# Experts' weights of a mixture-of-experts stage: transfers of 1 MB into twelve slots in place of 2 MB into six pairs of slots

## The reference, cut to what matters

```python
def moe(h, router_w, router_b, w1, w3, w2):
    ...
    out = gates[:, 0:1] * swiglu(t, w1[0], w3[0], w2[0])
    for e in range(1, N_EXPERTS):
        out = out + gates[:, e:e + 1] * swiglu(t, w1[e], w3[e], w2[e])
```

## Time and profile before

| | us |
|---|---|
| median of 3 runs | 1326.77 |
| lowest and highest | 1325.58, 1328.07 |
| the profiled execution | 1325.2 |
| its span, first to last instruction | 1323.4 |

### The profile page before, as it was taken

One profiled execution on the slowest core, in us unless ns is written; L12 is line 12 of the kernel. 1 busy time (PEld: TensorE's weight loads), 2 busy tenths in 40 slices (PEclk: granted clock), 3 DMA queues, 4 the chain that ended last, 5 costly groups with the idle time before them and its releaser, 6 DMA issues.

```text
span 1323.4 us, 40419 instructions
## 1 busy us (share of the span) xinstructions
PE 1225.4 (93%) x19184; PEld 918.4 (69%) x19184; DVE 354.2 (27%) x641; ACT 228.7 (17%) x307; POOL 17.8 (1%) x33
## 2 busy tenths in 40 slices
PE   4999999999989799999999999998779999999675
PEld 4889999999979768986555666664445666665343
DVE  3658664555454431001100000010001010001022
ACT  2434352333332210011000001000000000000001
POOL 0200000000000000000000000000000000000100
PEclk8999999999999799999999999999999999999999
DMA  9957678654556779999999999999999999999993
GB/s 387 356 188 285 270 298 330 260 178 176 188 223 257 285 280 405 403 410 429 424 426 425 424 425 424 425 424 427 426 425 425 425 419 417 415 414 415 425 425 165
DMA packets 44149, 470.73 MB, mean 356 GB/s; under 512 B 5140, under 2 KB 7736, under 8 KB 9544
## 3 DMA queue, kind: packets, MB, share of 16 engines
q1 hardware_dynamic: 42192, 462.83, 85.1%
q0 software_dynamic: 1392, 4.89, 1.1%
q10 hardware_dynamic: 392, 0.35, 0.1%
HBM read 463.99 MB, written 4.06 MB: 354 GB/s over the span
## 4 chain that ended last, share of the span: by engine, by line
PE 79%; DMA 16%; DVE 2%; issue 1%; ACT 1%; ACTq 0%; SPq 0%; POOL 0%; DVEq 0%; POOLq 0%
PE ps L485 78%; DMA raw<-moe_stream 14%; DMA raw<-dense_stream 1%; DMA hT<-in_norm_g 1%; DVE w_lo L1286 1%; PE ps L596 0%; ACT w_hi L1096 0%; PE ps L498 0%; PE ps L670 0%; DVE hT L1374 0%; DVE xT L1405 0%; ACTq L1108 0%; DVE tok L1814 0%; PE ps L908 0%; DVE xT L1535 0%
## 5 line engine op out<-in xcount | busy, mean ns | idle before, releaser
L485 PE MATMUL ps<-raw,hg 128*32 128x256 f32 x9408 | 522.3, 381 | 28.3 <-DMA raw<-moe_stream 28.3
L485 PEld LDWEIGHTS ps<-raw,hg 128*32 128x32 f32 x9408 | 326.7, 110 | 216.0 <-DMA raw<-moe_stream 22.3
L485 PE MATMUL ps<-rnd,w_hi 128*128 128x256 f32 x1632 | 299.8, 286 | 7.4 <-DVE rnd L1386 4.3
L485 PE MATMUL ps<-raw,arena 128*32 128x256 f32 x4704 | 265.2, 383 | 20.7 <-DMA raw<-moe_stream 20.7
L485 PEld LDWEIGHTS ps<-rnd,w_hi 128*128 128x128 f32 x1632 | 256.6, 194 | 11.4 <-issue 7.4
L485 PEld LDWEIGHTS ps<-raw,arena 128*32 128x32 f32 x4704 | 167.4, 111 | 114.1 <-issue 17.9
L485 PE MATMUL ps<-rnd,w_lo 128*128 128x256 f32 x816 | 232.5, 285 | 0.0
L1741 DVE TENSOR_TENSOR arena<-ps,arena 64x768 f32<-64x768 f32 (+1 forms) x48 | 41.3, 860 | 644.7 <-ACT arena L1209 644.7
L485 PEld LDWEIGHTS ps<-rnd,w_lo 128*128 128x128 f32 x816 | 158.1, 194 | 0.0
L1286 DVE TENSOR_TENSOR w_lo<-raw,w_hi 128x2048 fp32r<-128x2048 f32 x53 | 121.2, 2291 | 111.2 <-ACT w_hi L1096 111.2
L1209 ACT ACTIVATE arena<-ps 64x768 f32<-64x768 f32 (+1 forms) x56 | 40.4, 722 | 631.9 <-PE ps L485 631.9
(11 more groups left out here) (175 smaller groups left out, 402.9 us busy)
## 6 DMA issues: line engine op xcount, KB each, us to landing
raw<-moe_stream SPq DMA_DIRECT2D x168, 2048.0 KB, 22.3
raw<-dense_stream SPq DMA_DIRECT2D x101, 1024.0 KB, 7.9
y_rows<-arena SPq DMA_DIRECT2D x20, 96.0 KB, 13.0
out<-tok SPq DMA_DIRECT2D x2, 512.0 KB, 3.3
arena<-dft_constants POOLq DMA_DIRECT2D x1, 640.0 KB, 9.8
tok<-in_x_prompt SPq DMA_DIRECT2D x1, 512.0 KB, 4.6
tok<-in_x_sample SPq DMA_DIRECT2D x1, 512.0 KB, 5.7
arena<-bias_table POOLq DMA_DIRECT2D x1, 512.0 KB, 11.4
```

The costliest lines, as they stand in the source:

```text
L485: return pe.matmul(out, lhsT, rhs, start=first, stop=last, **kw)
```

## The change

The twelve slots are filled one by one: each piece is a transfer of its own, with a semaphore of its own. A piece's slot can be loaded again when that piece is used. In memory each piece is stored by itself, so that each partition reads 8 KB in one run. The order of slots in the buffers is the same as before, and so is the order of pieces. The first two pieces take the place of the first pair in the dense part, and the wait for the dense loads in `raw` is made slot by slot. The stores of result rows stand after the thirteenth transfer of a job, which is piece 12; before, they stood after the pair of pieces 12 and 13.

```diff
-PAIR = 2
-PAIR_SLOTS = 6
-RING = PAIR * PAIR_SLOTS
-MOE_LOADS = MOE_PIECES // PAIR
+RING = 12
...
-    moe_full = [sem(f"moe_full{i}") for i in range(PAIR_SLOTS)]
+    moe_full = [sem(f"moe_full{i}") for i in range(RING)]
...
+    RAW_ORDER = (4, 5, 0, 1, 2, 3)
...
-    def pair_slot(t):
-
-        k = t % PAIR_SLOTS
-        if k < PAIR_SLOTS // 2:
-            at = (2, 0, 4)[k]
-            return raw_2[:, at:at + PAIR, :]
-        at = (4, 0, 2)[k - PAIR_SLOTS // 2]
-        return raw[:, at:at + PAIR, :]
+    def piece_slot(t):
+
+        k = t % RING
+        return raw_2[:, (2, 3, 0, 1, 4, 5)[k], :] if k < RING // 2 else raw[:, RAW_ORDER[k - RING // 2], :]
...
-                t = MOE_LOADS * job + i // PAIR
-                pe.wait_ge(moe_full[t % PAIR_SLOTS], 16 * (t // PAIR_SLOTS + 1))
-                return pair_slot(t)[:, i % PAIR, :].rearrange("p (i n) -> p i n", i=2)
+                t = MOE_PIECES * job + i
+                pe.wait_ge(moe_full[t % RING], 16 * (t // RING + 1))
+                return piece_slot(t).rearrange("p (i n) -> p i n", i=2)
...
-                sp.dma_start(pair_slot(0), moe_stream[0, 0]).then_inc(moe_full[0], 16)
+                for t in range(2):
+                    sp.dma_start(piece_slot(t), moe_stream[t, 0]).then_inc(moe_full[t], 16)
...
-            for i in range(0 if job else 1, MOE_LOADS):
-                t = MOE_LOADS * job + i
-                if t < PAIR_SLOTS // 2:
+            for i in range(0 if job else 2, MOE_PIECES):
+                t = MOE_PIECES * job + i
+                if t < RING // 2:
                     sp.wait_ge(*used_up[N_SPLIT - 1])
-                elif t < PAIR_SLOTS:
+                elif t < RING:
                     for n in range(N_PRE - RAW, N_PRE):
-                        if n % RAW // PAIR * PAIR == (4, 0, 2)[t - PAIR_SLOTS // 2]:
+                        if n % RAW == RAW_ORDER[t - RING // 2]:
                             sp.wait_ge(*raw_free[n])
-                sp.wait_ge(e_used, PAIR * (t + 1))
-                piece = moe_stream[i, bass.ds(which, 1)].rearrange("o p a b n -> (o p) a b n") if e else moe_stream[i, 0]
-                sp.dma_start(pair_slot(t), piece).then_inc(moe_full[t % PAIR_SLOTS], 16)
-                if e and job < EXPERTS and i == PAIR_SLOTS:
+                sp.wait_ge(e_used, t + 1)
+                piece = moe_stream[i, bass.ds(which, 1)].rearrange("o p n -> (o p) n") if e else moe_stream[i, 0]
+                sp.dma_start(piece_slot(t), piece).then_inc(moe_full[t % RING], 16)
+                if e and job < EXPERTS and i == RING:
                     store_rows(job - 1)
...
-    moe = np.empty((MOE_LOADS, EXPERTS, P, PAIR, 2, HALF // 2), np.float32)
+    moe = np.empty((MOE_PIECES, EXPERTS, P, 2, HALF // 2), np.float32)
...
-        piece = moe[i // PAIR, :, :, i % PAIR]
+        piece = moe[i]
...
-    return pre, moe
+    return pre, moe.reshape(MOE_PIECES, EXPERTS, P, HALF)
```

More of the change, by code:

```diff
@@ L171 @@
 LAST_DOWN = max(n for n, piece in enumerate(PLAN) if piece[0] == "w2")
-assert MOE_PIECES % PAIR == 0 and len(MOE_PLAN) == MOE_PIECES
+assert len(MOE_PLAN) == MOE_PIECES
 ROWS = 4
```

## The result

The changed kernel takes 1331.55 us (median of 20 runs, 1328.15 to 1333.98); the kernel before, 20 runs beside it, 1326.74. The ratio is 1.0034, 95% interval 1.0027 to 1.0042: slower by 4.8 us. Predicted were 1333.0 us and +6.3. The profiled execution has a span of 1328.7 us, 5.3 more than before.

A forecast was written before the change was run, and what follows sets the result against it. Transfers were taken to bound the kernel from 585 us to the last landing at 1307.67 us. Terms +10.1 - 2.0 - 1.85 = +6.3 us gave 1333.0 us, range 1325.0 to 1338.0.

The forecast's parts named there:

- Row length: From 585 us to the last landing, 8 KB rows instead of 16 KB cost 1.4% of 722 us, +10.1 us.
- early dense window: In 12:36 us of the profile before, 8 KB rows of the dense stream saturated the engines at 420 GB/s.
- One transfer-bound stretch of 722 us: From 585 to 1307.67 us, the last landing, transfers set the pace throughout, in long jobs as in light ones.
- Slots one by one: In the first expert, slots returned one piece earlier let transfers run closer behind TensorE: -2.0 us, bounds 0 and -4.9.
- Tail: After the last landing TensorE has one piece left instead of two: -1.85 us, bound above 0.
- SyncE's work: 168 more issues at 0.40 us cost SyncE 67 us, inside its waits for TensorE of 739.9 us; priced at nothing.
- The cover: SyncE's 739.9 us of waits for TensorE hide the added issues; without it they would cost 67 us.
- B: Gain and loss cancel: short rows cost 0.2 to 0.9%, or less of the stretch counts; 1324.3 to 1329.4 us, chance 0.22.
- C: Row length costs nothing, so the lead and half tail remain: -3.85 us, 1322.9 us, chance 0.12.
- D: Each transfer's own cost comes through: 5% of a lone pair's 3.1 us uncovered gives 1349 us; chance 0.05.
- B's second half: Dips of slices 31 to 35 are a true TensorE limit, so 1.4% is lost over 557 us only, +7.8.
- C's rule: The Trainium skill asks for 128 partitions and at least 1 MiB per DMA for full bandwidth; both kernels keep to that.

The follow-up runs named there:

- The part alone: Kernel before with only the rows shortened: 168 transfers of 2 MB in pairs of slots, each partition's 16 KB as two 8 KB runs; 1337.26 us, ratio 1.0073.
- the pair kernels: Kernel before with first 56 pieces one by one, then 16 KB pairs; ratio 0.9990, with last pair one by one too 0.9972, with last six 0.9952.

## Why the prediction was right, step by step

**Row length, +10.1 us.** Shown. The part alone lengthened the stage by 10.9 us and the time by 9.8. In the changed kernel the windows fell from 427 to 420 and from 426 to 419 GB/s, as the row of the early dense window had said. The 1.4% was my choice between 0, 1.7 and 2.1%, and it was a good one: from 124 us after the stage's start to the last landing the mean is 419 GB/s before and 413 after.

**One transfer-bound stretch of 722 us.** Held as a whole: the 10.9 us that short rows alone added are 1.5% of it, and four of the seven later jobs are long ones. Had the long jobs kept TensorE's own pace, only the light ones would have grown, by under 5 us (an estimate: 1.6% of some 300 us). But the loss is not even. Before, then after, and the two deep dips after beside a calm stretch:

```profile
600.00:1300.00 700.00, 652.70 (x11680) 389.67 (x11680) 73.19 (x93) 46.64 (x66) 3.85 (x4) 0.99 1.00 422
600.00:1060.00 460.00, 435.26 (x7768) 259.93 (x7768) 42.86 (x56) 31.39 (x46) 0.00 (x0) 0.99 1.01 425
1060.00:1225.00 165.00, 164.00 (x3044) 98.97 (x3036) 16.12 (x20) 10.02 (x13) 0.00 (x0) 1.00 1.00 416
...
600.00:1300.00 700.00, 650.19 (x11606) 377.26 (x11605) 71.93 (x90) 46.16 (x65) 3.85 (x4) 1.00 1.01 417
600.00:1060.00 460.00, 435.87 (x7762) 254.41 (x7765) 42.88 (x56) 31.45 (x46) 0.00 (x0) 1.00 1.01 419
1060.00:1225.00 165.00, 162.11 (x2988) 96.22 (x2978) 14.73 (x18) 9.88 (x13) 0.00 (x0) 1.00 1.01 413
671.30:701.30 30.00, 30.00 (x560) 18.07 (x556) 3.86 (x4) 2.41 (x3) 0.00 (x0) 1.00 1.01 418
1102.60:1132.60 30.00, 30.00 (x560) 18.07 (x556) 3.86 (x4) 2.41 (x3) 0.00 (x0) 1.00 1.00 398
1211.40:1241.40 30.00, 22.31 (x372) 11.07 (x364) 4.04 (x6) 1.77 (x3) 3.46 (x4) 1.00 1.01 400
```

Up to 1060 us the rate falls by 1.4%, in the 165 us of the dips by 0.7%.

**Slots one by one, -2.0 us.** Right in kind and rather small. Between short rows in pairs and the changed kernel the stage shrinks by 3.5 us (2.3 against the second trace of the changed kernel), and 1.07 MB more is moved at the end of the first expert, 2.5 us. In the pair kernels the term was 2.3 to 2.9 us of stage. A piece landed 7.4 us after its issue in the median of 480:570 us, where I had said 7.6:

```profile
L1022 SPq DMA_DIRECT2D raw<-moe_stream x35: 327/328/356, 479.8 to 568.0; - x35
...
DMA to landing us min/median/max: 6.0/7.4/8.4
```

**Tail, -1.85 us.** 3.80 to 1.98, -1.82. It holds only because the transfers ahead of the last are single as well and TensorE waits for each of them. The prediction had only asked whether the piece before the last lands in time.

The measured terms give 10.9 - 3.5 - 1.8 = +5.6 against +6.3 predicted, +5.3 in the span (0.3 us less in the dense part) and +4.8 in the medians. That the sum came out so near is in part luck: I had the row term 0.8 us too small and the slots 0.3 to 1.5 us too small, and these two errors have opposite signs in it.

**SyncE's work, nothing.** The price was right as far as the runs show, its working was not: I had 0.40 us for each issue and 67 us in all. The wait of SyncE for TensorE fell from 739.9 us by far more:

```profile
SPq L1022 <- PE ps L479: 383.6, 217, 15.2
```

Most of those 356 us lie in issues that take longer: all expert issues together took 57 us before and 382 after. They cost the transfers no rate that the runs show: in 920:980 it is 420 GB/s with issues of 1992 ns in the median, and 420 with pairs of short rows, whose issues take 373 ns there.

```profile
L1022 SPq DMA_DIRECT2D raw<-moe_stream x37: 332/1992/4349, 904.8 to 992.0; - x37
...
L1031 SPq DMA_DIRECT2D raw<-moe_stream x12: 372/373/373, 922.8 to 979.0; - x12
```

So most of the 6% that the chain gives to SPq is time in which the engines were full anyway. The cover held, but it was half used up, not an eleventh.

**Against the rivals.** B (gain and loss cancel), C (row length is free) and D (each transfer's own cost) needed a rate loss under 0.9%, of none, or beyond 2.1%. It was 1.6% in 920:980, with a fixed part that goes with the packet. D is out also because 168 transfers with short rows ran at the 420 GB/s of 336. B's second half came true in part: its sign was that the dipping slices don't fall while the others do, and three of the five did not. The two deep dips after begin where SyncE issues the stores of result rows (1102.6 and 1211.4 us), but the stores at 671.3 us take it about as long, and 418 GB/s go on behind them. Pairs with short rows have the same two dips (401 and 408 GB/s in the 30 us from their stores), before has a shallower, longer one. They cost the changed kernel some 3 us (an estimate: 20 GB/s of 419 for twice 30 us). What causes the dips of either kernel was not tried. C's rule of at least 1 MiB in each DMA kept to, the row length still made the difference.

## What to carry to other kernels

When transfers set the pace, first look at the length of one row: at 128 partitions the rate was 406, 420, 426 and 429 GB/s for rows of 4, 8, 16 and 24 KB. The size of one transfer costs at two other places: at the last transfer, where compute must follow, and where compute is the bound for a while and the ring is a stock for later. Here long rows in the middle and short transfers only at those two places gave the fastest kernel; a slot more or less is worth its transfer time once (2.2 to 2.8 us here), not for each turn of the ring.

## What the runs showed of the hardware that I had not expected

- An issue on SyncE gets longer when much is queued: median 333 ns with pairs of 16 KB rows, 373 (at most 4472) with pairs of 8 KB rows, 1170 with twelve single transfers, 333 (at most 6126) with ten, and 2214 with twelve of 4 KB rows, 600 us onwards. With the number of transfers equal, shorter rows made it longer both times (six pairs of 16 KB rows against 8 KB, twelve pieces of 8 KB against 4 KB), so the packets waiting count, and not the transfers alone. Against that alone, six pairs of 8 KB rows have as many packets as twelve pieces, and a shorter median. That the queue holds so many packets and no more is my reading; its size was not measured.
- Transfers over 64 partitions each, by turns the lower and the upper half, moved half of what those over 128 do, 220 GB/s, with the engines' share at 1.01 and packets of 16 KB at 1.20 us. What the two halves share was not tried.
- A row of 24 KB went as one packet of 24 KB: 25.66 MB in the 1044 packets above.
